# One block pair after the other: a transformer pair with product-key experts, its dense work cut into two passes of two token blocks, with the expert gathers of the first pass beside the second

## What is computed

```python
def block(args):
    xb, eb, gb = args
    ub = jnp.take(u, eb, axis=0)
    hid = jax.nn.gelu(jnp.einsum('tkd,td->tk', ub, xb), approximate=False) * gb
    vb = jnp.take(v, eb, axis=0)
    return jnp.einsum('tk,tkd->td', hid, vb)
```

## Time and profile before

| | |
|---|---|
| time, median of 3 runs | 2741.86 us (2736.21 to 2760.91) |
| profiled execution, first to last instruction | 2733.2 us |
| median less that span | 8.7 us |
| PE busy | 2263.1 us, 83% |
| DVE busy | 1475.1 us, 54% |
| POOL busy | 1188.2 us, 43% |
| ACT busy | 645.8 us, 24% |
| moved by DMA | 665.46 MB, of it 536.94 MB by gathers |
| mean granted TensorE clock | 0.935 |

### The profile page before, as it was taken

How to read it: one execution, slowest core, us unless ns; L and a number is a source line. 1 busy time by engine, 2 the same in 40 slices (tenths; PEclk the granted TensorE clock), 3 DMA queues, 4 the chain that set the end, 5 groups by cost and what they waited for, 6 DMA issues and landing times.

```text
span 2733.2 us, 27506 instructions
## 1 busy us (share of the span) xinstructions
PE 2263.1 (83%) x9564; PEld 1445.1 (53%) x9564; DVE 1475.1 (54%) x3398; ACT 645.8 (24%) x1548; POOL 1188.2 (43%) x1128
## 2 busy tenths in 40 slices
PE   7999999999999999896977776767777777676775
PEld 6876888889979877665532222322223222232222
DVE  2435232375573425779866664557654567644434
ACT  3225332421120435422121111111111211111111
POOL 5200222110000221325566666666676666766664
PEclk9999999999999999898989998999988999988899
DMA  4211131144452222048889999999999999999998
GB/s 140 78 47 63 63 123 70 70 175 173 186 201 91 78 78 78 32 175 311 310 333 354 359 363 363 367 367 355 363 374 354 358 379 364 373 364 367 372 362 308
DMA packets 170936, 665.46 MB, mean 243 GB/s; under 512 B 19632, under 2 KB 20160, under 8 KB 160320
## 3 DMA queue, kind: packets, MB, share of 16 engines
q0 software_dynamic: 147456, 536.94, 52.1%
q1 hardware_dynamic: 23360, 127.00, 12.7%
HBM read 661.76 MB, written 2.10 MB: 243 GB/s over the span
## 4 chain that ended last, share of the span: by engine, by line
PE 42%; POOL 20%; DVE 15%; issue 10%; another core or an unknown queue 9%; ACT 2%; DMA 1%; SPq 0%; POOLq 0%; DVEq 0%; ACTq 0%
POOL area L544 11%; PE bank L1034 9%; PE bank L1035 9%; PE bank L1036 9%; POOL weights L535 8%; DVE weights L1925 6%; PE bank L1489 4%; PE bank L1076 2%; PE bank L1132 2%; PE bank L1187 1%; PE bank L1206 1%; PE bank L1093 1%; PE bank L1115 1%; PE bank L1099 1%
## 5 line engine op out<-in xcount | busy, mean ns | idle before, releaser
L1431 PE MATMUL bank<-area,gain_row 128*128 128x512 f32 x1888 | 967.3, 656 | 368.5 <-issue 204.2
L1431 PEld LDWEIGHTS bank<-area,gain_row 128*128 128x128 f32 x1888 | 366.6, 207 | 962.3 <-issue 824.1
L1925 DVE CUSTOM_DVE_ANT_0 weights<-weights,bank 128x1024 f32<-128x1024 f32 x504 | 596.9, 1218 | 346.7 <-DMA weights<-in_peer_u,scratch 241.0
L544 POOL DMA_INDIRECT area<-in_peer_v,scratch x512 | 491.5, 960 | 269.4 <-issue 142.3
L535 POOL DMA_INDIRECT weights<-in_peer_u,scratch x504 | 482.5, 957 | 261.4 <-issue 146.7
L918 ACT ACTIVATE gain_row<-ident,scratch 128x128 f32<-128x128 f32 x472 | 178.5, 398 | 1082.8 <-remote 588.7
L463 POOL CAST weights_split<-weights 128x2048 fp32r<-128x2048 f32 x25 | 47.7, 1906 | 851.1 <-DMA weights<-in_w_in 508.1
L1034 PE MATMUL bank<-h_T_high,weights_split 128*128 128x512 f32 (+1 forms) x544 | 211.6, 389 | 0.4 <-POOL weights_split L464 0.4
L1035 PE MATMUL bank<-h_T_low,weights_split 128*128 128x512 f32 (+1 forms) x544 | 209.7, 386 | 0.0
L1036 PE MATMUL bank<-h_T_high,weights_split 128*128 128x512 f32 (+1 forms) x544 | 209.7, 385 | 0.0
L1545 DVE CAST weights_split<-weights 128x2048 fp32r<-128x2048 f32 x41 | 50.4, 1228 | 209.0 <-DMA weights<-in_w_ff 122.8
(11 more groups left out here) (310 smaller groups left out, 3010.3 us busy)
## 6 DMA issues: line engine op xcount, KB each, us to landing
weights<-in_w_ff SPq DMA_DIRECT2D x32, 1024.0 KB, 4.8
scratch<-in_w_ada SPq DMA_DIRECT2D x48, 512.0 KB, 6.5
weights<-in_w_in SPq DMA_DIRECT2D x22, 1024.0 KB, 4.8
area<-in_w_pq SPq DMA_DIRECT2D x4, 2048.0 KB, 9.4
area<-in_peer_v,scratch POOLq DMA_INDIRECT x512
weights<-in_peer_u,scratch POOLq DMA_INDIRECT x504
weights<-in_w_mk SPq DMA_DIRECT2D x4, 1024.0 KB, 4.8
weights<-in_w_out SPq DMA_DIRECT2D x4, 1024.0 KB, 4.8
```

What stands on the lines that cost most here:

```text
L544: pool.indirect_dma_start(vring[k], None, A["peer_v"], index).then_inc(v_landed[k], 16)
L1431: ins = pe.matmul(bank[half][:], wdiag[:, (done + i) % 4, :], vring[r % RING][:, half * COLS:(half + 1) * COLS], start=(first and i == 0), ...
L1925: dve.tensor_tensor_reduce(out=up_slot(b, r), in0=up_slot(b, r), in1=token[b][:], scale=1.0, scalar=0.0, op0=ALU.mult, op1=ALU.add, accum_ ...
```

## The change

The dense work is done in two passes: the first over token blocks 0 and 1, the second over blocks 2 and 3. All 78 weight chunks of the layers are loaded and split in each pass, the output projection and the expert queries among them, which now also use three fp32r matmuls. Keys and values of the first pass are kept for the second; the memory's keys and values and some masks go to DRAM and back. `w_ada` and the memory projections are done in the first pass alone. Every matmul of a chunk has 256 columns.

- `W` has four slots of half a chunk. POOL splits the first half of each chunk, DVE the second (`feed`). A half waits for PE's end with the half four before it.
- The first pass runs alone. In the second, each engine's order is woven with the rows by `along`: a generator of the dense work gives, after each step, the number of rows that must have been issued by then, from a table of stage lengths (`STAGES`, `mark`), 232 of 512 rows within the pass. The rest follows after it.
- On POOL, before the split of chunk c the rows up to the mark of chunk c-1 plus 5 are issued.
- The rings have six slots for up rows and five for down rows, and `LAG` is 56. The token's rows are in SBUF (`token_rows`) in place of PSUM.
- In the first pass, SP issues two rows of `w_ada` ahead of each chunk of the feed-forward layer, through two slots; the code below shows what each waits for.
- Projections are no longer woven into attention.

```diff
-RING = 8
-TURNS = SLOTS // RING
-LAG = 88
-W_SLOTS = 3
+RU, RV = 6, 5
+LAG = 56
+ROWS = NB * SLOTS
+TAIL = SLOTS - LAG + 4
+W_SLOTS = 4
...
+FF_ORDER = [("f1", 0), ("f1", 1), ("f2", 0), ("f1", 2), ("f2", 1), ("f1", 3), ("f2", 2), ("f2", 3)]
+FF_ORDER = [(kind, 4 * r + j) for kind, r in FF_ORDER for j in range(4)]
...
+STAGES = [("mixn", 1, 10), ("in", 12, 70), ("fox", 20, 42), ("chk", 20, 38), ("y", 1, 9), ("out", 4, 23), ("post0", 1, 10),
+          ("memn", 1, 5), ("mq", 4, 23), ("mem", 12, 22), ("memy", 1, 5), ("mo", 4, 23), ("post1", 1, 10), ("ffn", 1, 5),
+          ("ff", 32, 186), ("post2", 1, 10), ("attn", 1, 6), ("in2", 10, 60), ("swa", 20, 28), ("gla", 10, 45), ("mixed", 1, 6),
+          ("out2", 4, 23), ("add", 1, 5), ("peern", 1, 8), ("wq", 8, 53)]
+LENGTH = sum(us for _, _, us in STAGES)
+ROWS_WITHIN = 232
...
+def mark(stage, i=0):
+    at = 0.0
+    for name, n, us in STAGES:
+        if name == stage:
+            return int((at + us * (i + 1) / n) * ROWS_WITHIN / LENGTH)
+        at += us
...
+        token = sb("token_rows", [P, 2, D])
...
+        def along(work, rows):
+            n = 0
+            for want in work:
+                while n < want:
+                    next(rows)
+                    n += 1
+            for _ in rows:
+                pass
...
+                if p == 0 and name in ("f1", "f2"):
+                    for r in range(rows, min(48, 2 * (c - ORD[0, "f1", 0] - 1))):
+                        if r >= 2:
+                            sp.wait_ge(ada_used, r - 1)
+                        sp.dma_start(ada[:, r % 2, :], A["w_ada"][r]).then_inc(ada_landed[r % 2], 16)
+                        rows = r + 1
...
+                for h, src in enumerate(halves(c)):
+                    w = 2 * c + h
+                    if w >= W_SLOTS:
+                        sp.wait_ge(w_used if w % 2 == 0 else tile_done, (w - W_SLOTS) // 2 + 1)
...
+            def down_row(n):
+                k, turn = n % RV, n // RV
                 if turn > 0:
                     pool.wait_ge(v_free[k], turn)
+                pool.indirect_dma_start(vring[k], None, A["peer_v"], index(n)).then_inc(v_landed[k], 16)
...
+            def parts_between():
+                last = mark("mixn")
+                for c in range(FIRST[1] + 1, len(ORDER)):
+                    _, name, i = ORDER[c]
+                    stage, at = ("ff", FF_ORDER.index((name, i))) if name in ("f1", "f2") else (name, i)
+                    yield last + 5
+                    split(c)
+                    last = mark(stage, at)
+            def rows():
+                for n in range(ROWS + LAG):
+                    if n >= LAG:
+                        down_row(n - LAG)
+                    if n < ROWS:
+                        up_row(n)
+                    yield
+            split(FIRST[1])
+            along(parts_between(), rows())
...
+            def tokens(key, ps, x=(HTH, HTL), start=True, stop=True, turn=None):
+                c = ORD[key]
+                for h in range(2):
+                    w = arrived(2 * c + h)
+                    for b in range(2):
+                        for k in range(4):
+                            kk = 4 * h + k
...
+                            ins = three(ps[:, b * T:(b + 1) * T], [t[:, kk, b * P:(b + 1) * P] for t in x],
+                                        [t[:, k * HALF:(k + 1) * HALF] for t in w], start and kk == 0 and b == 0, stop and kk == KT - 1 and b == 1)
+                    ins.then_inc(w_used if h == 0 else tile_done, 1)
...
+            def rows():
+                for n in range(ROWS + LAG):
+                    d = n - LAG
...
+                        pe.wait_ge(wdiag_ready, i + 1)
+                        pe.wait_ge(v_landed[d % RV], 16 * (d // RV + 1))
                         for half in range(2):
+                            ins = pe.matmul(bank[half][:], wdiag[:, i % 4, :], vring[d % RV][:, half * COLS:(half + 1) * COLS],
+                                            start=(r == 0), stop=(r == SLOTS - 1))
+                        ins.then_inc(v_free[d % RV], 1)
+                    yield
...
+            def feed(c):
+                while fed[0] < min(c + 1, len(ORDER)):
+                    w = 2 * fed[0] + 1
+                    fed[0] += 1
+                    raw, high, low = parts(w)
+                    dve.wait_ge(w_landed[w % W_SLOTS], 16 * (w // W_SLOTS + 1))
                     link(dve.tensor_copy(high, raw))
...
+                    feed(ORD[p, kind, f] + 1)
+                    if kind == "f1":
+                        hidden_split(p, f)
+                    if p == 0:
...
+                        if 1 <= t < 25:
+                            modulate(2 * t - 2)
+                            modulate(2 * t - 1)
...
+                    yield mark("ff", t)
...
+            def hidden(n):
+                b, r, k = n // SLOTS, n % SLOTS, n % RU
...
+                dve.wait_ge(u_landed[k], 16 * (n // RU + 1))
+                dve.tensor_tensor_reduce(out=uring[k], in0=uring[k], in1=token[:, b % 2, :], scale=1.0, scalar=0.0,
                                          op0=ALU.mult, op1=ALU.add, accum_out=hid[:, r:r + 1]).then_inc(u_free[k], 1)
...
+            along(work(1), rows())
```

More of the change, by code:

```diff
@@ L30 @@
 NB = TOK // P
+T = 2 * P
 D = 1024
@@ L663, in attention, with norm @@
+            def norm(p, n, s):
+                for b in range(2):
+                    act.wait_ge(x_ready, X_AT(p, s, b))
+                    squares(n, b, X[:, 2 * p + b, :])
+            def attention(p, lo, hi):
+                G = U_END * p
                 for u in range(lo, hi + 4):
@@ L1007, in _ @@
+            act.activation(fsq[:, i:i + 1], fsq[:, i + 1:i + 2], ACT.Sqrt, scale=1.0 / D, bias=fsq[:, i:i + 1]).then_inc(fin_rms, 1)
         @block.tensor
         def _(pe):
[L1009 to L1017 removed]
@@ L1518, in _ @@
+            for _ in work(0):
+                pass
+            along(work(1), rows())
         @block.vector
```

2618 lines of the change are left out of this document (1224 added, 1394 removed).

## The result

The changed kernel takes **3723.7 us** (3720.6 to 3730.0, 4 runs) against 2745.4 (2736.2 to 2760.9, 4 runs) of the kernel before: ratio 1.357, 95% interval 1.351 to 1.362. The forecast was 3350 with a range up to 3480. The direction was right, the time is 374 us more than forecast and outside the range.

The account below looks back on a forecast made before the run. It took PE to bound the dense part and transfers the rows. First pass 917, second pass 1510, rows alone 897 and tail 18 sum to 3342; with 8.7 us between span and median, 3350 us, range 2860 to 3480.

Parts of the forecast that it names:

- part 4: Second pass after the lag: POOL's split waits behind gathers needing PE's last row sums; 59 chunks cost 920 us.
- POOL's split is not late: Rival, chance 0.15: POOL splits while PE still works, so the second pass takes 1082 us and the kernel 2923.
- The chunk inside that round, 5.7: Second pass: PE's 48 matmuls of 256 columns for one weight chunk take 5.7 us, at 0.119 us each.
- 1620: Second pass, upper end: landing slowed beside gathers, or a PE clock of 0.90, gives some 1620 us against 1510.
- The gathers inside it, 2 x 2.48: Second pass, chunk with two rows: POOL's two pairs of gathers before its split take 2 x 2.48 us.
- 15.9: Second pass after the lag: a chunk with two rows takes 15.9 us, its matmuls, first row, gathers and split together.
- Projections "in", 113: Second pass, 12 chunks with up rows alone: POOL's late split makes them 9.4 us each, 113 us.
- Attention beside rows, 143: Second pass, fox and chk stages: 80 us of attention plus DVE's 26 rows and 1.6 picks make 143 us.
- First pass, `w_ada` 139 (120 to 163): First feed-forward stretch: serial loading of chunks and `w_ada` rows makes 24 rounds of 11.5 us, adding 139 us.
- Rows alone, 897 at 1.48: After the second pass: the 606 remaining gathers, 1.48 us apart, take 897 us (873 to 939).
- the second pass hides in its transfers: Rival, chance 0.10: the second pass takes only its transfers' 810 us, so the kernel takes 2651 us.
- `w_ada` is no circle: Rival, chance 0.10: first-pass rounds with `w_ada` take 5.7 us, 139 us off, so the kernel takes 3211 us.
- DVE and POOL exclude each other: Rival, chance 0.10: rows and splits on the two engines wait for each other, so the kernel takes 3460 us.

Follow-up runs that it names:

- experiment 5: Changed kernel with no row woven into the second pass, all rows after it, token rows of blocks 2 and 3 in PSUM: 3375.1 us, ratio 1.237.
- Experiment 4: Changed kernel with 56 further matmuls of 256 columns on TensorE ahead of most chunks of the second pass: 3679.7 us, ratio 1.337.
- fill_attn: Changed kernel with 4 further 512-column matmuls ahead of each unit's scores in the first two attention stages of each pass: 3662.2 us on another chip, ratio 1.412.
- experiment 8: Changed kernel with the token rows of blocks 2 and 3 in PSUM in place of SBUF: 3691.9 us, ratio 1.353.
- experiments 5 to 7: Three edits of the changed kernel: no rows in the second pass, 3375.1 us; `w_ada` left out, 3494.8; weights asked for ahead of `w_ada` rows, 3551.2.
- experiment 10: Two edits of the changed kernel: 56 matmuls ahead of the first attention stage, ratio 1.361; 4 of 512 columns ahead of each unit's scores, ratio 1.412.

## Why the prediction was wrong, point by point

Two terms failed: the price of a chunk in the second pass (5.7 us forecast, 8.0 measured, because after the wait ahead of it TensorE runs at 1.2 GHz for much of the chunk), and the length of a round with `w_ada` in the first (11.5 forecast, 15.3 measured). The structure of both, one wait behind the other, was right. Against the sum 917 + 1510 + 897 + 18 the trace has some 1055 + 1730 + 918 + 17. Of the 374 us, 138 are the first pass, 220 the second, 21 the rows; the 5 us less between span and median go the other way.

- **POOL's split stands behind PE's last rows** (part 4, the case forecast): right, as mechanism and in its place. The two waits on the page, the step of 3.2 us in the median round for one pair of gathers and the 580 for two rows show it. The rival "POOL's split is not late" was close as the price of its removal: 1082 forecast for the second pass, 1154 measured with the split two rows earlier.
- **The chunk inside that round, 5.7**: the step that failed. I took the earlier trace rows, a matmul in a stretch where PE never stopped, for a chunk that starts after a wait of 7 us. Without waits it is 5.8 (experiment 5); in this loop it is 8.5 in the round shown and 8.0 in the mean. I had allowed for 0.90 of the clock, from the rows' stretch, and only as an upper end (1620); the trace has 0.79. Experiment 4 shows that the wait makes it.
- **The gathers inside it, 2 x 2.48**: 5.65, since one or two of the four run beside VectorE's operations on two SBUF inputs (1.36 and 1.45). I had priced that for the rows alone and not here. Chunk +2.8, gathers +0.7, first sum +0.4 and split +0.2 are the 4 us between 15.9 and the 19.9 of the round shown. The forecast's 59 chunks have a mean of 15.6 (920 / 59), the 31 rounds of the feed-forward layer one of 19.5; these 31 alone make 120 of the 199 by which all that follows attention exceeded its 1241.
- **Projections "in", 113**: 148. The same order counts there: either earlier place of the split takes some 30 us off. Attention beside rows, 143: 137, but the number is right by luck. The sum put VectorE's rows and picks on top of 80 us of attention at full clock; in the trace PE is busy 134 of the 137 us at half clock, so two errors cancel.
- **First pass, `w_ada` 139 (120 to 163)**: the circle is there and costs 228. A round is 16.2 where shown and 15.3 in the mean, and not 11.5. From the end of its first product (551.6) to the next cast VectorE goes 9.7 us, where the sum had 1.2 + 1.1 + 5.3 = 7.6: SP's issues take 2.4 (551.70 to 554.1) and not 1.1, and VectorE's half lands some 7.2 after them and not 5.3, while the second product runs beside the issues; its half split took 4.1 where it had 1.8, the cast alone 2.8 where half of the earlier trace rows is 0.6, held up by POOL's subtraction of the other half; the hidden split is 1.3 in such a round, not 0.9. I had added the durations as if the two engines didn't meet, having named their rule for the rows. The rest of the pass, 766 to the first gather, was 811: 45 short. Its attention at half clock may be among the reasons, but no run prices it alone: with the clock at 1.00 (fill_attn) the added matmuls took what it gave.
- **Rows alone, 897 at 1.48**: 918 for 612 gathers (the sum had 606), 1.50 each, inside the stated bounds; the reason given, two SBUF inputs in VectorE's row, is shown by experiment 8.
- **The rivals**: that the second pass hides in its transfers, or that `w_ada` is no circle, is out (experiments 5 to 7). That DVE and POOL exclude each other was given 0.10 as a case by itself; it was no other case but a part of this one, and in the rounds with `w_ada` it went into the halves of a chunk, which the case had not named there.
- **The range**: it ended at 3480 because its bounds were taken one at a time from undisturbed rows. All its upper ends at once (950 + 1620 + 939 + 18 + 9 = 3536) would still have fallen 188 short, since both failed terms lie above their own upper ends. The three misses (clock, landing, shared access to SBUF) are all of one kind, a duration read where its engine had company of another sort, and they all go up.

What stays open: why the attention stages of the changed kernel run at 0.50 and those of the kernel before at 1.00, both with PE busy nearly throughout. Two windows of the kernel before:

```profile
160.00:200.00 40.00, 40.00 (x274) 32.35 (x273) 13.51 (x40) 11.56 (x36) 0.00 (x0) 1.00 0.15 53
240.00:280.00 40.00, 38.66 (x225) 26.74 (x223) 22.88 (x117) 25.55 (x77) 0.00 (x0) 1.00 0.05 14
```

A difference that stands in the list of the change is the nearest rival: its projections are woven into attention. In the first window 143 of its matmuls are a projection's (L1034 to L1036, 256 or 512 columns), much like the wide matmuls that experiment 10 put in. In the second there is none, and the clock holds at 1.00 all the same, coming from 1.00. Bf16 mask matmuls are no difference, as both kernels have them (L1096, 32 of them from 93 to 216 us, there), and wider scores don't do it alone, as the changed kernel's second pass has scores of 384 and 512 columns and stays at 0.50 (1211 to 1361 us). Whether the weave is what counts was not tried.

## To carry to other kernels

When work is woven between two engines by hand, write down for each queue what stands ahead of the step that the other engine needs, and ask whether that in turn waits for the other engine's last step: here one number, 5 or 3, was worth 580 us. A duration taken from a stretch in which the engine never waits does not hold for a loop in which it waits each time; price the clock with the wait (here 5.8 us a chunk without waits, 8.0 with them). And halving a job between two engines that read SBUF together can give nothing where the halves meet: 4.1 us for VectorE's half beside POOL's, 3.8 for both halves on VectorE alone.

## What the runs showed of the hardware that was not expected

- An idle time of 7.8 us ahead of each chunk brought TensorE to 1.2 GHz for some 6 of the 8.5 us of the chunk shown (8.0 in the mean of the chunks of that stretch, 5.8 without waits and 5.9 with the wait filled), and filling it brought 2.4 GHz back. Where rounds were 10 us with PE busy 92%, the clock stood at 0.99.
- PE busy by the profile does not keep the clock up: attention ran at 0.50 with 134 of 137 us busy, fell back there from a burst ahead of it, and ran at 1.00 in the first pass (0.74 to 0.87 in the second) once 4 matmuls of 512 columns stood ahead of each unit.
- VectorE's cast of 128x1024 took 0.69 us alone and 2.8 beside POOL's subtraction from two SBUF tiles (2.34), and, in the run with the split two rows earlier, a row product with two SBUF inputs 3.36 in place of 1.22. The Trainium skill, "SBUF — State Buffer", section "Who interferes with whom", has the one that issues first block the other for its whole length; by this rule the trace agrees for the cast and the row product.
